# Weight splits closer to their use, first tiles K by K, norm halves on GpSimd, and an unread product, in a two-block transformer kernel

## The reference, cut to what matters

```python
h = h + hybrid_mixer(rmsnorm(h, norm_mix), w_in, ..., w_out)
#   v = sc_b * causal_dwconv(sc_c * sc_u, sc_conv_w)        (short convolution)
h = h + memory_cross_attention(rmsnorm(h, norm_xa), rmsnorm(mem, mem_norm), w_q, w_k, w_v, w_o)
h = h + (silu(hn @ w_gate) * (hn @ w_up)) @ w_down          (hn = rmsnorm(h, norm_ffn))
x = rmsnorm(h, norm_final)                                  (end of block one)
qkv = rmsnorm(x, attn_norm_2) @ w_qkv_2                     (three attentions, w_o_2)
g = causal_dwconv_2(hn @ w_gate_2, conv_w_2, conv_b_2);  x = x + (silu(g) * (hn @ w_up_2)) @ w_down_2
return rmsnorm(x, final_norm_2)
```

## Time and profile before

| | |
|---|---|
| median of 3 runs | 2726.88 us |
| the profiled execution | 2727.17 us |
| its span, first to last instruction | 2725.1 us |
| granted TensorE clock | 0.999 |
| TensorE matmul busy | 2705.3 us, 99% |
| VectorE, ScalarE, GpSimd busy | 1936.4, 1297.2, 84.0 us |

### The profile page before, as it was taken

The page is one execution under the profiler, slowest core; times in us unless marked ns, Lnnn a source line. Parts: engine busy times, 40 slices in busy tenths (PEclk is TensorE's granted clock), DMA queues, the critical chain, the costliest instruction groups (busy, mean ns, idle before and its releaser), DMA issues.

```text
span 2725.1 us, 37306 instructions
## 1 busy us (share of the span) xinstructions
PE 2705.3 (99%) x15262; PEld 2331.2 (86%) x15262; DVE 1936.4 (71%) x2405; ACT 1297.2 (48%) x1652; POOL 84.0 (3%) x61
## 2 busy tenths in 40 slices
PE   8999999999999999999999999999999999999998
PEld 7888888888898888888888888888888888888887
DVE  7777888886768665666566785777787757775775
ACT  5444456755545443444344544645544434443444
POOL 1000000012101000000000110000000000000000
PEclk9999999999999999999999999999999999999999
DMA  6555555446556865555555655454555665565554
GB/s 244 189 185 185 178 165 177 146 164 217 185 170 177 202 211 193 189 191 188 191 187 186 197 181 179 148 170 153 177 185 189 192 194 172 187 203 194 177 187 157
DMA packets 139465, 501.46 MB, mean 184 GB/s; under 512 B 15384, under 2 KB 17440, under 8 KB 139040
## 3 DMA queue, kind: packets, MB, share of 16 engines
q1 hardware_dynamic: 136224, 491.67, 54.6%
q10 hardware_dynamic: 3072, 7.42, 2.0%
HBM read 495.36 MB, written 3.67 MB: 183 GB/s over the span
## 4 chain that ended last, share of the span: by engine, by line
PE 96%; DVE 2%; ACT 1%; DMA 1%; issue 0%; POOL 0%; DVEq 0%; ACTq 0%; POOLq 0%
PE PS L496 96%; DVE wlo L1265 1%; DMA raw<-in_w_in 0%; ACT whi L840 0%; DVE H L1259 0%; DVE AR L1275 0%; DMA XG<-in_x 0%; POOL AR L1811 0%; PE PS L579 0%; PE PS L746 0%; DVE XG L1732 0%; PE PS L652 0%; PE PS L723 0%; ACT AR L1122 0%; PE PS L622 0%
## 5 line engine op out<-in xcount | busy, mean ns | idle before, releaser
L496 PE MATMUL PS<-H,whi 128*128 128x512 f32 x5072 | 1791.6, 398 | 9.1 <-DVE wlo L1766 7.3
L1265 DVE TENSOR_TENSOR wlo<-raw,whi 128x1024 fp32r<-128x1024 f32 x929 | 1128.7, 1232 | 620.7 <-ACT whi L840 618.5
L840 ACT ACTIVATE whi<-raw 128x1024 fp32r<-128x1024 f32 x929 | 974.3, 1058 | 984.6 <-PE PS L496 880.4
L496 PE MATMUL PS<-H,wlo 128*128 128x256 f32 x5072 | 1414.8, 279 | 0.0
L496 PEld LDWEIGHTS PS<-H,whi 128*128 128x128 f32 x5072 | 952.9, 188 | 241.2 <-issue 9.0
L496 PEld LDWEIGHTS PS<-H,wlo 128*128 128x128 f32 x5072 | 956.3, 189 | 3.8 <-issue 3.4
L496 PE MATMUL PS<-Y,whi 128*128 128x512 f32 (+1 forms) x1408 | 474.1, 387 | 0.8 <-DVE XG L1732 0.5
L496 PE MATMUL PS<-Y,wlo 128*128 128x256 f32 x1344 | 373.9, 278 | 0.0
L496 PEld LDWEIGHTS PS<-Y,whi 128*128 128x128 f32 x1408 | 260.0, 188 | 59.1 <-issue 2.1
L496 PEld LDWEIGHTS PS<-Y,wlo 128*128 128x128 f32 x1344 | 253.0, 188 | 0.5 <-issue 0.2
L496 PE MATMUL PS<-whi,Y 128*128 128x512 f32 x704 | 216.8, 389 | 0.0
(11 more groups left out here) (188 smaller groups left out, 1082.8 us busy)
## 6 DMA issues: line engine op xcount, KB each, us to landing
raw<-in_ffn SPq DMA_DIRECT2D x528, 512.0 KB, 4.5
raw<-in_w_in SPq DMA_DIRECT2D x177, 512.0 KB, 4.4
raw<-in_w_qkv SPq DMA_DIRECT2D x96, 512.0 KB, 3.7
raw<-in_w_out SPq DMA_DIRECT2D x64, 512.0 KB, 4.2
raw<-in_w_o SPq DMA_DIRECT2D x40, 512.0 KB, 3.6
raw<-in_w_q SPq DMA_DIRECT2D x8, 512.0 KB, 4.4
raw<-in_w_k SPq DMA_DIRECT2D x8, 512.0 KB, 4.1
raw<-in_w_v SPq DMA_DIRECT2D x8, 512.0 KB, 4.6
```

What stands on the lines that cost most here:

```text
L496: return e.matmul(out, l, r, start=start, stop=stop)
L840: a.then_inc(e.activation(c.whi[:, s % NW, :], c.raw[:, s % NRAW, :], ACT.Copy), "whi")
L1265: v.then_inc(e.tensor_tensor(c.wlo[:, s % NW, :], c.raw[:, s % NRAW, :], c.whi[:, s % NW, :].bitcast(F32), ALU.subtract), "wlo")
```

## The change

- ScalarE splits sub `t // 2 + 4` in slot t, VectorE sub `t // 2 + 3`, instead of 5 for both. The preambles end one and two splits earlier.
- `HELD` is gone; the stages in it, and `su`, `xo`, `ao2`, take their first tile K by K.
- GpSimd adds the two 256-column halves of each norm's sum; TensorE's product and VectorE's mean are over 256 columns, in one instruction each.
- Side tasks move: `xs` 0 by two slots, `mcol` (two tiny products) from six slots into the stage `wo2`'s last part to 6 slots ahead of `wv`, `norm` 3 and `mid` by one slot.
- `pace`: a float32 product of 256 columns, whose result nothing reads, in the first slot of the gate tiles 8 and 16 of the second block.

```diff
+HI_AHEAD, LO_AHEAD = NW - 1, NW - 2
-HELD = ("wq", "g0", "qa", "g1", "d00", "d01", "d02")
+BY_K = ("su", "wq", "xo", "g0", "d00", "d01", "d02", "qa", "ao2", "g1")
 def walk(stage, j, K, m):
-    if stage in ("su", "xo", "ao2") and j == 0:
+    if stage in BY_K and j == 0:
         return [(i, k) for k in range(K) for i in range(m)]
-    cut = K - 2 if stage in HELD and j == 0 else K
-    return [(i, k) for part in (range(cut), range(cut, K)) for i in range(m) for k in part]
+    return [(i, k) for i in range(m) for k in range(K)]
...
-    out += [(END[NUM["xs", j]] // 4, "xs", j) for j in range(8)]
+    out += [(END[NUM["xs", j]] // 4 + 2 * (j == 0), "xs", j) for j in range(8)]
-    ... (first_slot("wo2") + 38, "mcol", 0)]
+    ... (first_slot("wv") - 6, "mcol", 0)]
-    out += [(a + 4, "norm", 3), (a + 7, "mid", 0), (a + 28, "norm", 4), ...]
+    out += [(a + 5, "norm", 3), (a + 8, "mid", 0), (a + 28, "norm", 4), ...]
+    out += [(BEGIN[NUM["g1", j]] // 4, "pace", j) for j in (8, 16)]
...
-        p.wait_ge("sum_add", 7 * n + 7)
-        p.then_inc(mm(bank, c.ones, c.SUM, True, True), "norm_sum")
+        p.wait_ge("sum_half", n + 1)
+        p.then_inc(mm(bank[:, 0:T], c.ones, c.SUM[:, 0:T], True, True), "norm_sum")
...
+    def pace(_):
+        p.then_inc(mm(take("pace", _, "b")[:, 0:T], c.ones, c.tri[:, 0:T], True, True), "pace")
+        yield
...
-            split(t // 2 + NW)
+            split(t // 2 + HI_AHEAD)
...
-            split(t // 2 + NW)
+            split(t // 2 + LO_AHEAD)
...
-        v.then_inc(e.tensor_scalar(m, bank[:, 0:T], 1.0 / 2048, eps, ALU.mult, ALU.add))
-        v.wait_ge(*v.at)
-        v.then_inc(e.scalar_tensor_tensor(m, bank[:, T:2 * T], 1.0 / 2048, m, ALU.mult, ALU.add), name)
+        v.then_inc(e.tensor_scalar(m, bank[:, 0:T], 1.0 / 2048, eps, ALU.mult, ALU.add), name)
...
+        if i == 7:
+            g.wait_ge("sum_add", 7 * n + 7)
+            g.then_inc(e.tensor_tensor(c.SUM[:, 0:T], c.SUM[:, 0:T], c.SUM[:, T:2 * T], ALU.add), "sum_half")
```

More of the change, by code:

```diff
@@ L178, in tasks @@
     out += [(after("z") - 2 + 12 * g, "grp", g) for g in range(4)]
-    out += [(first_slot("wo2") + 14, "msq", 0), (first_slot("wo2") + 32, "mnorm", 0), (first_slot("wo2") + 38, "mcol", 0)]
+    out += [(first_slot("wo2") + 14, "msq", 0), (first_slot("wo2") + 32, "mnorm", 0), (first_slot("wv") - 6, "mcol", 0)]
     q = first_slot("wq")
@@ L185, in tasks @@
     a = first_slot("qa")
-    out += [(a + 4, "norm", 3), (a + 7, "mid", 0), (a + 28, "norm", 4), (a + 32, "qa", 0), (a + 35, "rcol", 0)]
+    out += [(a + 5, "norm", 3), (a + 8, "mid", 0), (a + 28, "norm", 4), (a + 32, "qa", 0), (a + 35, "rcol", 0)]
     v = first_slot("ka")
@@ L235 @@
     "xt": [("b", 0, 2, "xt_copy", 1, 1)],
+    "pace": [("b", 0, 0, "pace", 0, 1)],
     "ssd": [("b0", 0, 2, "ssd_exp", 2, 1), ("b1", 0, 2, "ssd_exp", 2, 2), ("o", 6, 9, "ssd_z", 1, 1)],
@@ L316 @@
     "whi wlo sub_done acc0 acc1 h_hi h_made y_hi y_made cr "
-    "sq sum_add norm_sum norm_mean norm_root norm_ok "
+    "sq sum_add sum_half norm_sum norm_mean norm_root norm_ok "
     "msq madd mnorm_sum mnorm_mean mnorm_root mnorm_ok mcol_turn mcol_ok rcol_turn rcol_ok "
@@ L324 @@
     "stk_s stk_q stk_ln stk_m stk_c stk_z stk_exp stk_a stk_pv stk_sq stk_n stk_root stk_y "
-    "bnd_s bnd_max bnd_exp bnd_w bnd_turn bnd_copy bnd_pv bnd_sq bnd_n bnd_root bnd_y gain_x xt_turn xt_copy fgain half last_x fin_gain fsq fin_mean fin_root fin_ok"
+    "bnd_s bnd_max bnd_exp bnd_w bnd_turn bnd_copy bnd_pv bnd_sq bnd_n bnd_root bnd_y gain_x xt_turn xt_copy pace fgain half last_x fin_gain fsq fin_mean fin_root fin_ok"
 ).split()
@@ L529, in mnorm @@
         bank = take("mnorm", 0, "b")
-        p.wait_ge("madd", 7)
-        p.then_inc(mm(bank, c.ones, c.MSUM, True, True), "mnorm_sum")
+        p.wait_ge("madd", 8)
+        p.then_inc(mm(bank[:, 0:T], c.ones, c.MSUM[:, 0:T], True, True), "mnorm_sum")
         yield
@@ L755, in tensor_program @@
     side = Side({"norm": norm, "mnorm": mnorm, "mcol": mcol, "rcol": rcol, "sc": sc, "cb": cb, "dt": dt, "xs": xs, "ssd": ssd,
-                 "grp": grp, "xa": xa, "dfa": dfa, "dfb": dfb, "stk": stk, "bnd": bnd, "xt": xt})
+                 "grp": grp, "xa": xa, "dfa": dfa, "dfb": dfb, "stk": stk, "bnd": bnd, "xt": xt, "pace": pace})
     b = 0
@@ L1210, in scalar_program @@
             h0(k)
-        split(s)
+        if s < HI_AHEAD:
+            split(s)
     a.wait_ge("vec", 16)
@@ L1276, in conv, with mean @@
                        name if sh == width - 1 else None)
-    def mean2(m, bank, eps, name):
-        v.then_inc(e.tensor_scalar(m, bank[:, 0:T], 1.0 / 2048, eps, ALU.mult, ALU.add))
-        v.wait_ge(*v.at)
-        v.then_inc(e.scalar_tensor_tensor(m, bank[:, T:2 * T], 1.0 / 2048, m, ALU.mult, ALU.add), name)
+    def mean(m, bank, eps, name):
+        v.then_inc(e.tensor_scalar(m, bank[:, 0:T], 1.0 / 2048, eps, ALU.mult, ALU.add), name)
     def newton(r, m, u, rooted, n, name=None):
@@ L1297, in norm @@
         v.wait_ge("norm_sum", n + 1)
-        mean2(c.SUM[:, 0:T], bank, eps, "norm_mean")
+        mean(c.SUM[:, 0:T], bank, eps, "norm_mean")
         yield from idle(2)
@@ L1305, in mnorm @@
         v.wait_ge("mnorm_sum", 1)
-        mean2(c.MSUM[:, 0:T], bank, c.col("eps5"), "mnorm_mean")
+        mean(c.MSUM[:, 0:T], bank, c.col("eps5"), "mnorm_mean")
         yield from idle(2)
@@ L1462, in mid @@
                 yield
-        yield from idle(17)
+        yield from idle(16)
         v.wait_ge("norm_ok", 5)
@@ L1772, in vector_program @@
             lo0(k)
-        split(s)
+        if s < LO_AHEAD:
+            split(s)
     v.wait_ge("vec", 16)
@@ L1823, in msq @@
             g.then_inc(e.tensor_tensor(c.MSUM, c.MSUM, c.MSQ[i % 2], ALU.add), "madd")
+        g.wait_ge("madd", 7)
+        g.then_inc(e.tensor_tensor(c.MSUM[:, 0:T], c.MSUM[:, 0:T], c.MSUM[:, T:2 * T], ALU.add), "madd")
     def mid(_):
```

## The result

The changed kernel takes 2761.95 us in the median of 4 runs (2762.25, 2761.98, 2761.93, 2751.67); the kernel before, on the same chip, 2726.89. The ratio is 1.0119, 95% interval 1.0107 to 1.0131. The prediction was 2728.0 with a range of 2717 to 2742: wrong, by 34 us, and outside the range.

What follows compares the result with a forecast made beforehand. The prediction took TensorE as the bound, 99% busy at full clock with small waits. Gains of 13.8 us against costs of 14.6 gave +0.8 on 2727.2, so 2728.0 us, range 2717 to 2742.

Steps and rivals of the forecast that it cites:

- The rows DMA: First feed-forward, 858 to 958 us: loads beside eight `rel_rows` transfers land late; one or two short waits, +1.0 us.
- The rhythm is lost in the first feed-forward: Rival, chance 0.25: after a late load TensorE's blocks take 352.8 ns instead of 345.9 until near 1575 us: +12.4, 2740 us.
- sc: Tiles 1 to 7 of `sc`: `wlo` late behind the read-out, 1.3 us each, +9.1; tile 0 +0.3; rhythm +1.2.
- mid: Near 1595 us: the `wlo` behind the eight pairs of `mid` comes late, +3.0 us with the restart.
- Half norms: Seven norm products: 256 columns instead of 512 save 0.43 us each, -3.0 us.
- I let no product wait: At norms: GpSimd's added 1.0 us delays no product, since splits no longer hold ScalarE's squares, giving some 2 us back.
- Walk and moved tasks: First tiles K by K -1.2 us at `g0`; `xs` 0 -0.6; `mcol` -0.9; norm 3 in fast rhythm -0.4.
- Pace: Gate tiles 8 to 21, second feed-forward: two products cost +0.8, faster blocks give -6.1; sum -5.3 us.
- the rival that it does nothing: Rival, chance 0.05: the slow rhythm may belong to parts 1 and 2 themselves; 6.1 not gained, 2734 us.
- 0.3 us to spare: Gate tiles `g1`: the `wlo` behind each read-out comes just in time, 0 cost; rival that they stall, 0.08, 2744 us.
- Freed waits: New split distances free waits ahead of the attention (-1.0), at `xo` (-0.5 and -0.5) and the start (-0.3): 2.3 us.

Runs made afterwards that it cites:

- e9: Changed kernel, distances 4 and 3 kept, with five raw buffers instead of four and four `wlo` buffers instead of five: 2745.59 us, ratio 1.0059.
- e5: Changed kernel with only ScalarE's split back at five buffers ahead, VectorE's staying at three: 2872.73 us, ratio 1.0542.
- e3: Changed kernel with the eight `rel_rows` transfers issued 110 slots later, beside `d00` instead of `u0`, and twice as close: 2752.89 us, ratio 1.0102.
- e6: Changed kernel with VectorE's split at four buffers ahead instead of three, ScalarE's staying at four: 2732.42 us, ratio 1.0011.
- e4: Changed kernel with one more unread product of 256 columns, eight slots into `d00`: 2753.38 us, ratio 1.0096.
- e7: Changed kernel, VectorE making the next `wlo` before the read-out in the last slot of an `sc` tile: 2752.5 us, ratio 1.0084.
- e11: Kernel before with nothing but the half norms: 2724.86 us, ratio 0.9991.
- e8: Changed kernel with both splits five ahead, `mid` and norm 3 back in their old slots, and a `pace` product eight slots into `d00`: 2718.0 us, ratio 0.9969.
- e12: Kernel before with nothing but first tiles K by K, `xs` 0 two slots later and `mcol` moved to the attention's transposes: 2723.77 us, ratio 0.9988.
- e10: Kernel before with nothing but the two `pace` products: 2721.97 us, ratio 0.9981.
- e1: Changed kernel with both splits five buffers ahead again, all else of the change kept: 2719.62 us, ratio 0.9980.

## Why the prediction was wrong

**The step that failed** is "The rows DMA": "I take +1.0 for one or two short waits; 0 to +4". It measured seven waits and 13.8 us. Two things were wrong in it. It put the median 6.8 us of a load into a sum of which the slack was 0.2, where the load of the first wait took 9.2, 2.4 more, and those of the next ones 5.6 to 7.7. And it priced a late load only by its own `wlo`, while ScalarE takes its queue in order: the silu of the read-out stands behind the split that waits, VectorE's product behind the silu, and the `wlo` that TensorE wants behind that. At four of the seven waits the sub that TensorE wanted had its own load long before. The second error was there to be asked: the prediction says what a wait of VectorE holds, never what a wait of ScalarE for a load holds, and the change shortened every load's lead against ScalarE by a sub. e9 shows that one sub more of lead is enough, at no shorter a latency; e5 what one sub less does; e3 that in `u0` it takes the transfers as well; e6 that something other than a load can stand at the head of ScalarE's queue.

**The rhythm** was seen as a rival ("The rhythm is lost in the first feed-forward", 0.25, 12.4 us), and its mechanism and place came true, at 10.7. But 2740 left the price of the stalls out that turn it: the rival took a wait between 858 and 958 as a short one. With them it would have been 2753, 9 us short of the result; the rest lies in the other lines of the table, 3.5 of it in `wo1` to `xo` and 2.5 in the second feed-forward. e4 shows that it is a state that one product resets.

**sc**: right. A wait at each of the tiles 1 to 7, 35.9 us apart (34.1, the stall and the rhythm), at the sub named, costing 1.40 where 1.3 was worked out, and 0.3 behind tile 0 as worked out. The rhythm behind them cost 2.0, of which 1.2 was taken. e7 confirms the order as the cause.

**mid**: right, 3.4 for 3.0. **Half norms**: right by 0.43 at each where nothing else waits; 2.3 in all (e11) for 3.0. In the changed kernel TensorE doesn't wait at a norm product; with ScalarE's split at five it does (0.7 us in e11 and e8, 5.8 in e5), so "I let no product wait" holds only with that split nearer, as its reason had it. **Walk and moved tasks**: 3.4 alone (e12), 2.7 taken.

**Pace**: right as a mechanism, 5.2 alone (e10) for 5.3; the rival that it does nothing is out. e10 shows 348 matmuls in 60 us, where the same columns went at 340 in 60 (907 in 160) before. The Trainium skill ("TensorE: Matmul & The Clock Gate", section Back-to-back issue gap) gives the columns-alone gap that was set beside that rival for an isolated matmul; for a stream of weight loads and matmuls, which this is, it says that both ops set the spacing. Neither gives two spacings for the same stream, as e10 and the kernel before have them. The product was tried in three places and turned the rhythm in all; whether another short instruction would do as well wasn't tried. In the changed kernel it gave 2.8, since part 2 lost its rhythm to the wait at 2593. That is the "0.3 us to spare" of the gate tiles: it wasn't there once in 22 tiles, by 0.2 us, again behind a load that ScalarE waited for.

**Freed waits**: the 0.9 at line 652 went and 1.5 came in at the attention, but four short waits in `wo1` and `wq` (3.2 us) stand against it that no step had. The prediction looked for a thin slack in the stages where VectorE is full and passed over these. Three of the four are in e9 as well, so they are no load's. At the two longer ones of `wo1` VectorE works beside GpSimd. Its multiplication there, in another `wo1` tile and at the wait, with GpSimd's addition:

```profile
614.34 0.69 DVE L1266 TENSOR_TENSOR H<-AR,H 128x512 fp32r<-128x512 f32 x1 [0.70 <-ACT H L973]
583.42 1.37 DVE L1266 TENSOR_TENSOR H<-AR,H 128x512 fp32r<-128x512 f32 x1 [2.08 <-ACT H L973]
582.95 1.30 POOL L1848 TENSOR_TENSOR AR<-AR 128x512 f32<-128x512 f32 x1 [21.71 <-ACT AR L963]
```

**What stays open**: what decides between the two rhythms when TensorE restarts. The kernel before, e10, e11 and e12 never lost the one of the first feed-forward (62 runs in the last batch, by their times); by their times e1 lost it in 2 of 12, e6 in 10 of 12, e9 in 4 of 6, e7 in 3 of 4, the changed kernel in 3 of 4. The last wait in `u0`, at sub 316, left TensorE slow in the trace of the changed kernel and fast in that of e7. In e8 the slow stretch began with no late `wlo` at all. That the runs 10 to 14 us above the others are this is shown by traces for the changed kernel and e6 (slow) and e7 (fast), and inferred for the rest.

## What to carry to other kernels

Where one engine's step frees the buffer that a load fills, and another engine waits for that load in program order, the lead of the load is the buffers less the difference of the two distances. Here shortening the later engine's distance more than the earlier one's took a sub from it, and what stands behind the waiting instruction in its queue pays first. And a kernel that is 99% busy has stalls that cost more than their length: where a trace has two rhythms, count matmuls in windows behind each stall.

## What the runs showed of the hardware that I hadn't expected

A `rel_rows` transfer (192 KB, one row of 384 values to 128 places) keeps the 16 DMA engines 66.6% busy over 6 us at some 30 GB/s, and the 512 KB loads on another queue move nothing for 4.5 us of it; behind it they reach 437 GB/s.

An instruction of VectorE that reads two tiles of SBUF takes longer beside GpSimd's addition, up to three times as long: each of the 16 multiplications of `mid` in the kernel before took 0.47 to 1.52 us (median 0.48), and all of those over 1 us lie beside it.

In the changed kernel the granted clock fell once, apart from its start and end, behind the waits in `u0`. Windows of the changed kernel, columns as above:

```profile
949.00:953.00 4.00, 1.39 (x8) 1.00 (x7) 3.01 (x4) 2.80 (x4) 0.00 (x0) 1.00 0.82 127
953.00:956.40 3.40, 3.40 (x13) 2.92 (x12) 2.22 (x2) 0.00 (x0) 0.00 (x0) 0.50 0.76 75
956.40:960.00 3.60, 3.60 (x22) 3.16 (x21) 0.00 (x0) 0.00 (x0) 0.00 (x0) 1.00 1.01 353
```

TensorE was idle for 2.6 of the 4.0 us before; then 13 matmuls took 3.4 us at 1.2 GHz, where they take 2.1 at 2.4 GHz by the window behind (3.6 x 13/22). That is 1.3 us of the 4.4 which this stall cost. The three other stalls of over 2 us in `u0` left the clock full, so what decides isn't shown. In other runs it fell behind a single wait: of 1.8 us in e7, and of 2.1 us at `qa` in e1, where the +2.25 has some of it. Windows from 53 us in e7, and from that wait in e1:

```profile
53.20:56.60 3.40, 3.40 (x12) 2.86 (x12) 3.34 (x7) 0.28 (x1) 0.00 (x0) 0.51 0.76 236
1599.70:1604.00 4.30, 4.30 (x15) 3.70 (x16) 4.30 (x3) 2.04 (x3) 2.76 (x2) 0.60 0.49 156
```
